# Transpositions and score products one by one ahead of long products

## What is computed

```python
def first_block(x, positions, ...):
    h = x
    h = h + FFN_RES * swiglu(rms_norm(h, ffn1_norm[l]), ffn1_w_gate[l], ffn1_w_up[l], ffn1_w_down[l])
    h = h + hybrid_mixer(rms_norm(h, mix_norm[l]), positions, w_in[l], b_gate[l],
                         w_branch_moba[l], w_branch_sb[l], w_out[l])
    h = h + FFN_RES * swiglu(rms_norm(h, ffn2_norm[l]), ffn2_w_gate[l], ffn2_w_up[l], ffn2_w_down[l])
    return rms_norm(h, final_norm)

def second_block(x, ...):
    x = x + 0.5 * swiglu_ffn(x, ffn1_norm, ffn1_w_gate, ffn1_w_up, ffn1_w_down)
    (fq, fk, fv, ff, dq, dk, dv, iq, ik, iw, ga, gb) = split_columns(h @ w_in)
    o_a = fox_attention(fq, fk, fv, log_f)
    o_b = dsa_attention(dq, dk, dv, iq, ik, iw, rel_bias)
    merged = jax.nn.sigmoid(ga) * (o_a @ w_branch_a) + jax.nn.sigmoid(gb) * (o_b @ w_branch_b)
    x = x + merged @ w_out
    return x + 0.5 * swiglu_ffn(x, ffn2_norm, ffn2_w_gate, ffn2_w_up, ffn2_w_down)
```

## Time and profile before

| | |
|---|---|
| median of three runs | 1117.95 us (1117.8 to 1118.03) |
| profiled execution | 1117.82 us, its span 1116.0 us |
| TensorE busy | 1110.3 us, 99% of the span, 5854 products and transpositions |
| TensorE's weight loads | 944.4 us |
| VectorE, ScalarE busy | 786.0 us (70%), 621.3 us (56%) |
| granted TensorE clock | full speed in all 40 slices |

### The profile page before, as it was taken

The page is one execution under the profiler, slowest core; times in us unless marked ns, Lnnn a source line. Parts: engine busy times, 40 slices in busy tenths (PEclk is TensorE's granted clock), DMA queues, the critical chain, the costliest instruction groups (busy, mean ns, idle before and its releaser), DMA issues.

```text
span 1116.0 us, 14890 instructions
## 1 busy us (share of the span) xinstructions
PE 1110.3 (99%) x5854; PEld 944.4 (85%) x5854; DVE 786.0 (70%) x1112; ACT 621.3 (56%) x825; POOL 57.7 (5%) x105
## 2 busy tenths in 40 slices
PE   9999999999999999999999999999999999999998
PEld 8888888888888888888888888888888788888887
DVE  6777754766887677775477787557898686777752
ACT  6556542677566455564346556337787854656540
POOL 1000000100000000000000000021343000000000
PEclk9999999999999999999999999999999999999999
DMA  9765565644454656655565555557643455665550
GB/s 317 250 189 189 190 244 190 209 158 144 162 193 157 207 188 189 189 189 189 189 208 187 190 189 189 189 154 256 223 146 122 150 176 166 189 190 193 191 180 38
DMA packets 142581, 208.02 MB, mean 186 GB/s; under 512 B 9296, under 2 KB 100584, under 8 KB 142512
## 3 DMA queue, kind: packets, MB, share of 16 engines
q1 hardware_dynamic: 139408, 198.07, 54.1%
q0 software_dynamic: 3088, 9.00, 2.4%
q10 hardware_dynamic: 16, 0.00, 0.0%
HBM read 205.98 MB, written 2.65 MB: 187 GB/s over the span
## 4 chain that ended last, share of the span: by engine, by line
PE 96%; ACT 2%; DVE 1%; issue 1%; DMA 0%; SPq 0%; DVEq 0%
PE banks L1800 27%; PE banks L1686 16%; PE banks L1688 16%; PE banks L1687 16%; PE banks L1797 14%; PE banks L1758 1%; PE banks L2031 1%; PE banks L1708 1%; PE banks L1976 1%; ACT w_hi L751 0%; DMA raw<-in_ffn_w_gate 0%; PE banks L2061 0%; DVE w_lo L1138 0%; PE banks L2009 0%; PE banks L2058 0%
## 5 line engine op out<-in xcount | busy, mean ns | idle before, releaser
L1138 DVE TENSOR_TENSOR w_lo<-raw,w_hi 128x2048 fp32r<-128x2048 f32 x186 | 422.8, 2276 | 167.0 <-ACT w_hi L751 166.6
L751 ACT ACTIVATE w_hi<-raw 128x2048 fp32r<-128x2048 f32 x186 | 352.2, 1897 | 111.9 <-PE banks L1688 108.2
L1800 PE MATMUL banks<-xT,w_hi 128*128 128x512 f32 x1344 | 314.3, 390 | 0.0
L1800 PEld LDWEIGHTS banks<-xT,w_hi 128*128 128x128 f32 x1344 | 249.3, 188 | 49.8
L1797 PEld LDWEIGHTS banks<-xT,w_lo 128*128 128x128 f32 x1344 | 167.4, 191 | 4.1 <-DVE xg L1152 0.7
L1686 PE MATMUL banks<-w_hi,xT 128*128 128x512 f32 (+1 forms) x432 | 170.4, 394 | 0.0
L1797 PE MATMUL banks<-xT,w_lo 128*128 128x256 f32 x1344 | 169.8, 283 | 0.2
L1688 PE MATMUL banks<-w_hi,xT 128*128 128x512 f32 (+1 forms) x432 | 166.9, 386 | 0.0
L1687 PE MATMUL banks<-w_lo,xT 128*128 128x512 f32 (+1 forms) x432 | 166.7, 386 | 0.0
L1686 PE MATMUL banks<-w_hi,hT_hi 128*128 128x512 f32 x352 | 137.3, 390 | 0.0
L1688 PE MATMUL banks<-w_hi,hT_lo 128*128 128x512 f32 x352 | 137.0, 389 | 0.0
(11 more groups left out here) (315 smaller groups left out, 902.6 us busy)
## 6 DMA issues: line engine op xcount, KB each, us to landing
raw<-in_ffn_w_gate SPq DMA_DIRECT2D x88, 512.0 KB, 3.9
raw<-in_ffn_w_up SPq DMA_DIRECT2D x88, 512.0 KB, 4.9
raw<-in_ffn_w_down SPq DMA_DIRECT2D x88, 512.0 KB, 4.3
raw<-in_w_in SPq DMA_DIRECT2D x76, 512.0 KB, 4.5
raw<-in_w_out SPq DMA_DIRECT2D x16, 512.0 KB, 4.2
raw<-in_w_branch_moba SPq DMA_DIRECT2D x4, 512.0 KB, 4.2
raw<-in_w_branch_sb SPq DMA_DIRECT2D x4, 512.0 KB, 5.2
raw<-in_w_branch_a SPq DMA_DIRECT2D x4, 512.0 KB, 4.3
```

The source lines that it names most:

```text
L751: act.activation(w_hi[u % SLOTS][:, 0:n], raw[u % RAWS][:, 0:n], ACT.Copy).then_inc(hi_done, 1)
L1138: dve.tensor_tensor(w_lo[r][:, 0:n], raw[r][:, 0:n], w_hi[u % SLOTS][:, 0:n], ALU.subtract).then_inc(lo_done, 1)
L1800: m = pe.matmul(bank[b + s], mh, xT[:, k].rearrange("p a s -> p (a s)"), start=first, stop=k == KC - 1, skip_group_check=c == 0)
```

## The change

Only TensorE's list changes; its instructions are the same in kind and number. The functions that issue short ones (`turn_x`, `turn_hidden`, `spread_rows`, `turn`, `turn_probs`, `scores`, `turn_merged`) become generators that stop behind each, and the functions that issue long ones get `between(i)`, called ahead of long product i, which issues the next short one from some i on. In a slot the last short one stands ahead of the last long one.

```diff
-            def three(dst, st, hi, lo, mhi, mlo, start, stop):
+            def three(dst, st, hi, lo, mhi, mlo, start, stop, between=None, i=0):
 
+                if between:
+                    between(i)
                 pe.matmul(dst, st(hi), mhi, start=start, stop=False)
+                if between:
+                    between(i + 1)
                 pe.matmul(dst, st(hi), mlo, start=False, stop=False)
+                if between:
+                    between(i + 2)
                 return pe.matmul(dst, st(lo), mhi, start=False, stop=stop)
+
+            def spaced(short, first):
+
+                return lambda i: next(short, None) if i >= first else None
...
-                turn_x(ph, 1)
-                batch(0, 0)
-                for q in range(2, 4):
-                    turn_x(ph, q)
-                batch(0, 1)
-                batch(1, 0)
-                batch(1, 1)
+                for tt, hf in Q_FFN:
+                    short = turn_x(ph, 2 + hf) if tt == 0 else None
+                    batch(tt, hf, spaced(short, 8) if short else None)
...
-                if c == 1 and ph == "F2":
-                    spread_rows(ph)
-                pair_products(ph, c, 1, 1, False).then_inc(unit_used, 1)
+                turns = spaced(spread_rows(ph), 1) if c == 1 and ph in FIRST_OF else None
+                pair_products(ph, c, 1, 1, False, turns).then_inc(unit_used, 1)
...
-                turn_x(ph, 2)
                 pe.wait_ge(lo_done, u + 1)
                 pe.wait_ge(xT_hi_done, x0 + 2)
                 for p in range(2):
                     if p:
                         pe.wait_ge(gained, 4 * GAIN_OF[ph] + 4)
                     pair_products(ph, 0, 0, p, True)
-                turn_x(ph, 3)
                 pe.wait_ge(xT_lo_done, x0 + 2)
                 for p in range(2):
-                    m = pair_products(ph, 0, 0, p, False)
+                    short = turn_x(ph, 2 + p)
+                    m = pair_products(ph, 0, 0, p, False, spaced(short, 0))
...
-                        if d == NCH - 1 and q == 3 and ph in NEXT:
-                            turn_x(NEXT[ph], 0)
+                        turns = spaced(turn_x(NEXT[ph], q - 2), 2) if d == NCH - 1 and q >= 2 and ph in NEXT else None
...
+                def turns_of(slot):
+
+                    for it in ITEMS[b]:
+                        if it.kind == "SM" and slot - it.slot == SM_AT["turn"]:
+                            yield from turn_probs(it)
+                    for it in ITEMS[b]:
+                        if it.kind == "TR" and slot == it.slot:
+                            yield from turn(it)
+                        if it.kind == "CU" and slot == it.slot:
+                            sum_rows(it)
+                        if it.kind in ("SM", "SB", "IX") and slot == it.slot:
+                            yield from scores(it)
...
+                for slot in range(4, 44):
                     j, q = divmod(slot, 4)
+                    turns, first = turns_of(slot), max(0, 12 - count_turns(slot))
+
+                    def between(i):
+                        if i >= first:
+                            next(turns, False)
+
                     if j < PROJ:
-                        project(j, q // 2, q % 2)
-                    elif slot < 44:
-                        branch(0, q)
+                        project(j, q // 2, q % 2, between)
+                    else:
+                        branch(0, q, between)
+                    rest_of(turns)
...
-                turn_merged(0)
-                turn_merged(1)
-                branch(1, 3)
+                branch(1, 3, spaced(two_turned(turn_merged, 0), 0))
                 output(0, 0, 0)
-                turn_merged(2)
-                turn_merged(3)
-                output(0, 0, 1)
+                output(0, 0, 1, spaced(two_turned(turn_merged, 2), 0))
                 for n, hf in ((0, 1), (1, 0), (1, 1)):
                     output(n, hf, 0)
-                    if (n, hf) == (1, 1):
-                        turn_x(NEXT[ph], 0)
-                        turn_x(NEXT[ph], 1)
-                    output(n, hf, 1)
+                    turns = two_turned(lambda q: turn_x(NEXT[ph], q), 0)
+                    output(n, hf, 1, spaced(turns, 0) if (n, hf) == (1, 1) else None)
```

More of the change, by code:

```diff
@@ L1693, in rows, with four @@
                 return w_hi[u % SLOTS][:, o:o + n], w_lo[u % RAWS][:, o:o + n]
-            def four(u, tt, dst, k0, first, last, n=NB, hi=xT_hi, lo=xT_lo):
+            def four(u, tt, dst, k0, first, last, n=NB, hi=xT_hi, lo=xT_lo, between=None):
                 for k4 in range(4):
@@ L1699, in four @@
                     m = three(dst, lambda z, k=k0 + k4: z[:, k, tt * P:(tt + 1) * P], hi, lo, mh, ml,
-                              first and k4 == 0, last and k4 == 3)
+                              first and k4 == 0, last and k4 == 3, between, 3 * k4)
                 return m
@@ L1844, in first_chunk @@
                 pe.wait_ge(xT_lo_done, 4 * PREP_OF[ph] + quarters(ph).index((tt, hf)) + 1)
-                m = four(u, tt, bank[tt][:], 4 * hf, hf == 0, hf == 1)
+                m = four(u, tt, bank[tt][:], 4 * hf, hf == 0, hf == 1, between=between)
                 if tt == 1:
@@ L2078, in project @@
                             pe.wait_ge(gated, 2 * (j - 7))
-                    m = four(u, tt, bank[2 * (j % 2) + tt][:, 0:n], 4 * hf, hf == 0, hf == 1, n)
+                    m = four(u, tt, bank[2 * (j % 2) + tt][:, 0:n], 4 * hf, hf == 0, hf == 1, n, between=between)
                     if tt == 1:
@@ L2128, in turn_merged, with two_turned, output @@
                                            xg[:, tt, n * NB + k * P:n * NB + (k + 1) * P], ident)
[L2129 to L2131 removed]
+                        if k == 3:
+                            ins.then_inc(m_turned, 1)
+                        yield True
+                def two_turned(turn, q):
+                    yield from turn(q)
+                    yield from turn(q + 1)
+                def output(n, hf, tt, between=None):
                     u = u0 + 24 + 2 * n + hf
@@ L2134, in output @@
                     pe.wait_ge(mT_lo, 4 * b + Q_MIX.index((tt, hf)) + 1)
-                    m = four(u, tt, bank[2 * n + tt][:], 4 * hf, hf == 0, hf == 1)
+                    m = four(u, tt, bank[2 * n + tt][:], 4 * hf, hf == 0, hf == 1, between=between)
                     if tt == 1:
```

71 lines of the change are left out of this document (43 added, 28 removed).

## The result

The changed kernel takes 1128.98 us (median of 4 runs, 1128.93 to 1129.35), the kernel before 1117.99 us beside it (4 runs, 1117.80 to 1118.13). The ratio is 1.0099 [1.0082, 1.0117]: slower by 11.0 us, where I had forecast 7.7 with a range up to 1129.0. The profiled execution took 1128.96 us (span 1127.2).

What follows compares the result with a forecast made beforehand. TensorE, busy 1110.3 of 1116.0 us, was taken as the bound. Terms 2.8 + 2.8 + 1.9 + 0.3 gave +7.8 us on 1117.82, so 1125.6 us, range 1119.0 to 1129.0 (own case 1123.5 to 1127.5).

Steps and rivals of the forecast that it cites:

- The sign: Whole kernel: slower, given a chance of 0.84, against 0.10 for the same and 0.06 for faster.
- B: Start of F1 and F3: T2 and T3 among the high products delay ScalarE and VectorE; two seams, +2.8 us.
- C: Start of M1: T3 later for ScalarE, waits of 0.2 us and, at slot 10's first score, 1.7 us; +1.9 us.
- A: Spreading: short ones standing singly between long products keep their price and each pay 0.010 us, 279 times; +2.8 us.
- D: Ahead of M0, F2, M1: T0 moves four long pitches earlier and waits about 0.1 us each; +0.3 us.
- step E: Scores ahead of value products: one head's steps move by nearly the same amount; 0, between -0.8 and +1.5 us.
- upper bound of 3.5 us: Start of F1 and F3: the delay if all of the 3.15 us less the old 1.7 us is paid twice.
- The 0.2 us at slot 8: Start of M1: TensorE waits 0.2 us for VectorE's part, which ends at 766.2 us.
- more waits than I found: Rival: M1's fox heads have the tightest slacks; doubling C and taking step E's upper end gives 1129 us; chance 0.12.

Runs made afterwards that it cites:

- e4_narrow: Changed kernel with the two 128-column products of each softmax or indexer score item cut to 32 columns; 1129.33 us (1.0102).
- e1_slots: Changed kernel with the mixers' slot loop as before the change (short ones as runs behind the long products, value products ahead of scores); 1122.30 us (1.0041).
- e3_pairs: Changed kernel with only the start of F1 and F3 as before the change; 1126.20 us (1.0077).
- e15_m1_start: e10_seams with T0 to T3 around M1's start also as before the change; 1118.82 us (1.0009).
- e10_seams: Changed kernel with both the mixers' slot loop and the start of F1 and F3 as before the change; 1119.38 us (1.0014).
- e8_scale_first: Changed kernel with ScalarE scaling the next fox head's probabilities ahead of the copy of the turned ones and the end of the pair; 1128.07 us (1.0091).
- e2_order: Changed kernel with the new order in a slot kept, but all short ones as runs behind the twelve long ones; 1123.07 us (1.0048).
- e12_fox_slots: Changed kernel with slots 24 to 33 of M1 alone not spread; 1126.63 us (1.0079).
- e5_probs_last: Changed kernel, still spread, with the probabilities' transpositions behind the scores of the same slot; 1131.56 us, three runs within 0.2 us and one at 1129.73.

## Why the prediction was wrong, step by step

The sign held, and the waits of B and C were at their places. The sum was 7.8 us, and 11.1 were measured between the profiled executions. A to D came to 7.6 us in all (B's spreading counted under A, D taken as forecast), with 1.9 for C by luck; the rest, 3.5 us, is step E, which had been put at 0.

**A, spreading, +2.8 us.** Right in kind. A short one keeps the price of a load, 0.117 us against 0.109 in a run, and its streaming doesn't matter (e4_narrow). Its size is what the pauses leave. Slots of M1 without a pause of note grow by 0.05 us each: 0.38 in slots 11 to 18, 0.47 in slots 35 to 43. In M1's slots 19 to 34 the changed kernel loses 4.1 us, e1_slots 0.4; less 0.8 for spreading 2.9 are pauses. With 0.6 at slot 16 of M0 and 1.3 at slot 10 of M1 pauses are 4.8 of the slots' 6.7 us. That leaves 1.9 us for spreading; with 0.3 in the two starts and some 0.6 elsewhere it is 2.8 us, the forecast's.

**B, start of F1 and F3, +2.8 us.** Right: 1.5 us each by the table, 2.8 us by e3_pairs, with the spreading in it. (Its upper bound of 3.5 us doesn't follow from its own terms, which give 2 x 1.45.) e11_t2_ahead puts T2 back and lets T3 stand one by one from the first high product on.

> The changed kernel with T2 ahead of the low products again at the start of F1 and F3, and T3 one by one among the high ones, but from the first of them on and not from the ninth. Theory of step B (what costs is that T3's copy on ScalarE is 3 us late): T3 ends some 2.3 us earlier than in the changed kernel, 0.8 us later than before the change, inside the slack; both waits go, 1129.0 - 2.7 = 1126.3 us, as with the whole start undone. Rival (T2's lateness counts as much, or any transposition among the high products does): 1127.5 us or more.

Measured: 1126.41 us (1.0077 [1.0063, 1.0091]), as with the whole start undone. So what costs is the place of T2 and T3, and not that T3 stands between products. The run moves both, and can't tell which: by the rows T2, taken out of a wait, makes some 0.5 us of each start, and T3's late copy the 0.5 us at the second half and the 0.3 us at the row spreading. My account had T2's part only in where the high products start (381.3, and 382.55 - 1.2 came of it).

**C, start of M1, +1.9 us.** The wait at slot 10 was there, with 1.3 us where I had 1.7, and two errors in it. The keys' remainder ended at 775.90 + 0.86 = 776.76; less the 3.2 us lost before it is 0.5 us later than the 773.04 of before, not 1.6. And the score was asked for at 775.31 + 0.23 - 3.2 = 772.3, not 772.9. So more than half of this wait is early asking, and less than half ScalarE's lateness. The 0.2 us at slot 8 was not there. At the turned keys 0.56 us came up that I hadn't followed so far (e15_m1_start). That both make up my 1.9 us is luck.

**D, T0 ahead of M0, F2 and M1, +0.3 us.** T0 stands at 191.10 us, in a trace that is 0.1 us ahead there, against 191.20 forecast. The wait at it is small, and no run parts it from the rest of the 1.5 us that e10_seams keeps; the 0.3 us are neither shown nor refuted.

**E, scores ahead of value products, 0.** Here it failed: 0 forecast, with 1.5 us at most, and 3.5 measured in pauses, 0.6 in M0 and 2.9 in M1. I had written that scores and probabilities move by nearly the same amount, "so the distance between them, which the other engines need, changes by under 1.5 us either way". That is the distance along one head. I hadn't looked at what the value products release. They end a wait on ScalarE, behind which the next head's scaling is queued, and their distance to the transposition that needs this scaling fell from 3.6 to 1.3 us. That is 1.3 us in three slots, by what e8_scale_first gains in them. The rest of the 2.9 us lies at the second fox head and the scores at 819 and 860 us, all asked for up to 2.6 us earlier than before; that it comes from early asking is shown for the slots together (e2_order, e12_fox_slots), not for each wait. The 0.6 us in M0 is the wait of the earlier trace rows, which I had counted among those that E could lengthen but left at 0. My rival "more waits than I found" named this stretch and gave 1129 us; I gave it a chance of 0.12. Its place was right. Its number is luck: it doubled C, which came to 1.9 us and not 3.8, and took 1.5 us for E. I had that upper end from single moves, not from a list of every slot.

## What to carry to other kernels

When instructions move on the engine that bounds, measure two distances for every slot: from each result to the instruction that asks for it, and from each instruction that frees a buffer to the next thing that is queued behind that wait on the other engine. A tight stretch has many small slacks, so a move by one slot's length costs at most of them at once; list them all before any is put at 0. And here a short instruction with weights of its own cost a load wherever it stood, 0.11 us in a run and 0.117 between long ones: putting it between long ones hid nothing. What it can hide in is a wait, as T2 did at F1's start, so look for that before it is moved.

## What I had not expected of the hardware

The long wait in e5_probs_last (slot 16 of M0) was followed by a lower clock. Windows of core 0 (TensorE busy, loads busy, and so on; the granted clock stands behind POOL), e5_probs_last and then the changed kernel:

```profile
243.00:246.00 3.00, 0.79 (x5) 0.40 (x4) 2.96 (x6) 2.96 (x5) 0.00 (x0) 1.00 0.79 249
246.00:250.00 4.00, 4.00 (x16) 3.13 (x16) 0.93 (x6) 1.67 (x5) 0.00 (x0) 0.62 0.20 75
```

```profile
243.00:246.00 3.00, 1.83 (x11) 1.35 (x10) 2.87 (x7) 2.98 (x4) 0.00 (x0) 1.00 0.88 294
246.00:250.00 4.00, 4.00 (x22) 3.42 (x21) 2.85 (x8) 4.00 (x11) 0.00 (x0) 1.00 0.11 42
```

After a pause of 2.2 us, with TensorE busy for 0.79 of 3 us, the granted clock of the next 4 us is 0.62: for most of them it is at 1.2 GHz and not at 2.4. In the changed kernel TensorE was busy for 1.83 us of the same 3, and the clock stayed at 1.00. Long product 1200, behind the wait, starts 1.5 us later than in the changed kernel (0.4 of them from before the slot), and 1212 starts 3.0 us later, though TensorE is busy all the time between them: a long and a short one take 0.64 us there and not 0.34. Over a whole run this shows as a mean granted clock of 0.998 in the three runs near 1131.6 us and 1.000 in the one that took 1129.73 us: there the clock held.
